# Second MLP in two phases, seven block products in both, hidden outputs in DRAM, low parts of the weights on GpSimd

## The chip, the cores and the metric

One core of a Trainium2 chip. The metric is the device time of one execution in microseconds; three runs of the kernel before gave 2306.87, 2307.96 and 2309.41 us, median 2307.96.

## What is computed

A trunk of two layers on x (1024 tokens by 1024 channels, float32). Only the end of layer 2 concerns this change:

```python
h = rms_norm(x, norm2_gain[i]) * (1 + scale2) + shift2
x = x + gate2 * squared_relu_mlp(h, mlp_w1[i], mlp_w2[i])
# squared_relu_mlp: jnp.square(jax.nn.relu(h @ w1)) @ w2, w1 is 1024x4096, w2 is 4096x1024
```

## The kernel before

All tensors lie with channels on the 128 partitions and tokens along the free dimension: `x` is 8 blocks of 128 channels by 1024 tokens. A float32 product is made of three matmuls on operands rounded to float32r: high part of the weights by high part of the input, high by low, low by high. ACT makes a high part (a copy to float32r), and POOL (GpSimd) or DVE makes the low part as the float32 value less the high one. `T.matmul` always has a 128x128 weight block and 512 tokens (a half).

A "unit" is 128 output channels: 8 blocks of input by 2 halves by 3, so 48 matmuls (`products`, L1564). The hidden layer of 4096 is worked in four groups of 1024 channels, each as two half-groups (`half_group`, L1909). A half-group computes four units of the hidden layer plainly (192 matmuls), squares them (`quad`, L1342), and multiplies these 512 hidden channels by w2 into x: for each of four pairs of output blocks (`DOWN_PAIRS`) seven block products instead of eight (`down_products`, L1874), each 2 weight blocks by 3 matmuls, so 168. The seven products are those of Winograd's form of Strassen's algorithm: quadrants of weights, B11 and so on of the input, and sums of them (S of weights, T of inputs). DVE adds each product as it ends into `x` (`down_evacuate`, L1389). POOL makes the four sums of weight quadrants and all low parts (`down_sums`, L455, `down_low`, L470). Weights come by SP's queue into two slots of `w_raw`.

The second MLP has no other work in it; the last half-group (`end=True`) is written out by hand. Before it `closing` (L1002) normalises the tokens and writes `h_hi` and `h_lo`; the end is SP's store of `out` (L424).

## Time and profile before

| | |
|---|---|
| median of three runs | 2307.96 us |
| profiled execution, its span | 2306.2 us |
| PE busy, matmuls | 98%, 10252 |
| DVE, ACT, POOL busy | 55%, 31%, 35% |
| second MLP, start to last matmul | about 1632 to 2301 us |
| PEclk in it | full speed |

The span runs from the first to the last instruction; the runs are timed around it, so they lie some 2 us above. A DMA row gives the time from issue to landing. PE's matmuls overlap in their pipeline: what one costs is the distance between starts, not its duration. A waiting engine is charged to whoever released it last.

### The profile page before, as it was taken

The numbers are of one execution on the slowest core, as the hardware profiler recorded it, in microseconds if no ns is written. First come the engines' busy times: TensorE is split into PE (matmuls) and PEld (weight loads), VectorE is DVE, ScalarE is ACT, GpSimd is POOL, SyncE is SP. The second block draws the span as 40 slices with busy tenths as digits, with TensorE's granted clock in tenths as the row PEclk, the third lists the DMA queues.
The fourth block names the chain that finished last, engine by engine and source line by source line (L and its number), as shares of the span: only waits on it lengthen the run. The fifth ranks groups of instructions, "written<-read, shape, count | busy, mean of one in ns | idle before, by whom it ended". The sixth has DMA issues, their size and how long they took to land.

```text
span 2306.2 us, 29119 instructions
## 1 busy us (share of the span) xinstructions
PE 2270.8 (98%) x10252; PEld 1812.3 (79%) x10252; DVE 1279.7 (55%) x1641; ACT 711.8 (31%) x978; POOL 803.4 (35%) x622
## 2 busy tenths in 40 slices
PE   7999999999999999999999999999999999999999
PEld 4786787888888888787888888888788888888887
DVE  8689687565565554564334421456554455545455
ACT  4328433223223222233222211224323323322322
POOL 0124403464454452301221112121154455355355
PEclk7999999999999999999999999999999999999999
DMA  6363521212212313223334221222111111111112
GB/s 259 121 185 88 210 92 70 86 55 82 86 51 83 99 55 101 86 87 119 129 118 133 84 72 46 83 73 91 56 49 43 55 55 40 51 55 45 46 64 92
DMA packets 84299, 201.38 MB, mean 87 GB/s; under 512 B 23937, under 2 KB 29953, under 8 KB 83714
## 3 DMA queue, kind: packets, MB, share of 16 engines
q1 hardware_dynamic: 65826, 139.70, 18.9%
q10 hardware_dynamic: 18400, 60.69, 7.5%
q8 instruction: 47, 0.77, 0.1%
q14 instruction: 26, 0.21, 0.0%
HBM read 182.54 MB, written 16.78 MB: 86 GB/s over the span
## 4 chain that ended last, share of the span: by engine, by line
PE 59%; issue 34%; POOL 5%; DVE 0%; POOLq 0%; ACT 0%
PE pp L1570 36%; PE pp L1894 23%; POOL w_lo L432 4%; POOL pr L446 1%; PE pp L1701 0%; POOL w_lo L473 0%; DVE w_lo L1024 0%; PE pp L1680 0%; POOLq L499 0%; DVE x L1398 0%; PE pp L1710 0%; POOLq L431 0%; DVE c_f L1353 0%; ACT w_hi L742 0%; ACT root L533 0%
## 5 line engine op out<-in xcount | busy, mean ns | idle before, releaser
L432 POOL TENSOR_TENSOR w_lo<-w_raw,w_hi 128x1024 fp32r<-128x1024 f32 x136 | 329.9, 2425 | 1186.8 <-ACT w_hi L518 1186.8
L1570 PE MATMUL pp<-h_hi,w_hi 128*128 128x512 f32 x1824 | 602.7, 400 | 15.5 <-DVE h_lo L1166 6.2
L1570 PE MATMUL pp<-h_lo,w_hi 128*128 128x512 f32 x1824 | 594.6, 396 | 0.0
L1570 PE MATMUL pp<-h_hi,w_lo 128*128 128x512 f32 x1824 | 594.5, 396 | 0.0
L1398 DVE SCALAR_TENSOR_TENSOR x<-pp,mod,x 128x512 f32<-128x512 f32 x392 | 294.4, 751 | 278.0 <-PE pp L1894 278.0
L1570 PEld LDWEIGHTS pp<-h_hi,w_hi 128*128 128x128 f32 x1824 | 339.2, 188 | 105.9 <-DVE h_lo L1052 12.9
L1570 PEld LDWEIGHTS pp<-h_hi,w_lo 128*128 128x128 f32 x1824 | 343.2, 188 | 83.2
L1570 PEld LDWEIGHTS pp<-h_lo,w_hi 128*128 128x128 f32 x1824 | 343.3, 188 | 81.2
L518 ACT ACTIVATE w_hi<-w_raw 128x1024 fp32r<-128x1024 f32 x162 | 171.5, 1058 | 615.2 <-PE pp L1570 448.0
L1894 PE MATMUL pp<-c_hi,w_hi 128*128 128x512 f32 x784 | 310.1, 396 | 0.4 <-DVE x L1398 0.4
L1894 PE MATMUL pp<-c_hi,w_lo 128*128 128x512 f32 x784 | 310.1, 396 | 0.0
L1894 PE MATMUL pp<-c_lo,w_hi 128*128 128x512 f32 x784 | 310.1, 395 | 0.0
L473 POOL TENSOR_TENSOR w_lo<-s_w,w_hi 128x768 fp32r<-128x768 f32 x112 | 143.6, 1297 | 135.3 <-ACT w_hi L742 135.2
L1346 DVE SCALAR_TENSOR_TENSOR c_f<-pp,tmp 128x512 f32<-128x512 f32 x84 | 55.5, 688 | 235.9 <-ACT tmp L749 233.5
L1894 PEld LDWEIGHTS pp<-c_hi,w_hi 128*128 128x128 f32 x784 | 147.3, 188 | 36.4 <-issue 0.8
L1894 PEld LDWEIGHTS pp<-c_lo,w_hi 128*128 128x128 f32 x784 | 147.3, 188 | 35.7
L1894 PEld LDWEIGHTS pp<-c_hi,w_lo 128*128 128x128 f32 x784 | 147.3, 188 | 35.6
L473 POOL TENSOR_TENSOR w_lo<-w_raw,w_hi 128x256 fp32r<-128x256 f32 x112 | 114.3, 1020 | 121.2 <-ACT w_hi L742 117.9
L742 ACT ACTIVATE w_hi<-s_w 128x768 fp32r<-128x768 f32 x112 | 70.9, 634 | 238.7 <-PE pp L1894 177.5
L1570 PE MATMUL pp<-hid_hi,w_hi 128*128 128x512 f32 x384 | 142.3, 398 | 1.6 <-POOL w_lo L432 1.6
L1570 PE MATMUL pp<-hid_hi,w_lo 128*128 128x512 f32 x384 | 141.6, 395 | 0.0
L1570 PE MATMUL pp<-hid_lo,w_hi 128*128 128x512 f32 x384 | 141.5, 395 | 0.0
(185 smaller groups left out, 2207.6 us busy)
## 6 DMA issues: line engine op xcount, KB each, us to landing
w_raw<-weights SPq DMA_DIRECT2D x218, 512.0 KB, 3.6
mod_t<-mod_w ACTq DMA_DIRECT2D x64, 512.0 KB, 4.1
mod_first<-mod_w SPq DMA_DIRECT2D x16, 512.0 KB, 15.3
mod_late<-mod_w ACTq DMA_DIRECT2D x2, 4096.0 KB, 23.3
v_dram<-v_out ACTq DMA_DIRECT2D x16, 512.0 KB, 5.5
vf<-v_dram ACTq DMA_DIRECT2D x16, 512.0 KB, 3.3
x<-x_in SPq DMA_DIRECT2D x4, 1024.0 KB, 8.1
qf<-q_dram SPq DMA_DIRECT2D x32, 128.0 KB, 2.5
```

Of the source, the lines that this page charges most:

```text
L432: nc.gpsimd.tensor_tensor(out=w_lo[:, s, :, :], in0=w_raw[:, s, :, :], in1=w_hi[:, s, :, :].bitcast(f32), op=ALU.subtract).then_inc(lo_don ...
L446: nc.gpsimd.tensor_tensor(out=pr[:, b, :, 0:P], in0=pr[:, b, :, 0:P], in1=small[:, b, 3, :].unsqueeze(2).to_broadcast([P, 4, P]), op=ALU.m ...
L473: nc.gpsimd.tensor_tensor(out=down_target(w_lo, part, end), in0=down_source(part, q), in1=down_target(w_hi, part, end).bitcast(f32), op=AL ...
L518: nc.scalar.activation(w_hi[:, s, :, :], w_raw[:, s, :, :], ACT.Copy).then_inc(hi_done, 1)
L742: nc.scalar.activation(down_target(w_hi, part, end), down_source(part, q), ACT.Copy).then_inc(d_hi, 1)
L1346: V.scalar_tensor_tensor(out=out, in0=src[:, columns_of(half)], scalar=0.0, in1=tmp[:, s, columns_of(half)], op0=ALU.max, op1=ALU.mult).th ...
L1398: V.scalar_tensor_tensor(out=xn, in0=banks[BANK[t]], scalar=mod[:, 6 * layer + GATE2, 2 * q + m:2 * q + m + 1], in1=xn, op0=ALU.mult, op1= ...
L1570: last = T.matmul((pp[s] if tile is None else tile)[:, cs], w[:, s, k, :], r[:, k, cs], start=(k == 0 and w is w_hi and r is hi), stop=(k ...
L1894: last = T.matmul(banks[BANK[t]], w[:, slot, k, :], r[:, i, OPERAND[t], :], start=(t in FRESH and i == 0 and w is w_hi and r is c_hi), sto ...
```

## The change

The second MLP is cut in two phases. The first computes the whole hidden layer, all 16 pairs of units (j = 0 to 15), and the second multiplies by w2. Pairs 0 and 1 are computed plainly, as before; pairs 2 to 15 (n = 0 to 13) by seven products, each of 4 weight blocks by 3 matmuls. Then come 16 pairs n = 14 to 29 for w2, four for each group of 1024 hidden channels, again by seven products of 12 matmuls.

The seven input combinations are kept as float32, high and low part. In the first phase they come from h (`combine_inputs`: one DVE instruction on 2048 elements per partition and twelve on 512, all with two inputs in SBUF). A pair's result is squared and combined to the seven inputs of the second phase, each stored to DRAM (`hid_dram`, 256 KB each, `save_pair`) and, at the start of each group, loaded again (`group_operand`): seven loads of 1 MB in pieces of 2 KB, issued by ACT at the seven products of the pair before (n = 13, 17, 21, 25). Each load overwrites the low part that the product has just finished with; ACT then makes the high part and DVE the low part in place (`operand_low`), 2048 elements per partition each.

A pair's weights are 1 MB in four quadrants of 256 KB in `w_raw`. POOL makes four sums and seven low parts, each of 512 elements per partition, in the order: sum S3, low parts 5 and 6 of the pair before, low 0, sums S1, S2, S4, low parts 1 to 4. `w_hi` and `w_lo` hold four products' weights. The quadrant A22 of the next pair is loaded only when low part 6 has been made, and S1 needs it.

In the first phase ACT also copies three partial products out of PSUM and makes three relus for each pair. The loops are written out; the first MLP is unchanged. `scaled` of the last normalisation writes a tile of its own (`g_f`), so it no longer waits for the low part two blocks back.

```diff
+O_B11, O_T1, O_T2, O_B22, O_T3, O_B21, O_T4, O_B12 = range(8)
+OUTPUTS = 7
+QUADS = 4
+UP_PAIRS = MLP_GROUPS * QUADS
+PLAIN_PAIRS = 2
+FAST_UP = UP_PAIRS - PLAIN_PAIRS
+FAST_PAIRS = FAST_UP + MLP_GROUPS * DOWN_PAIRS
+A11, A12, A21, A22 = range(4)
+S_1, S_2, S_4, S_3 = range(4)
+SUM_OF = {S_3: 1, S_1: 2, S_2: 3, S_4: 4}
+PLACED = ((0, 0, 0), (1, 0, 0), (1, 4, 1), (0, 4, 1), (1, 0, 1), (0, 4, 0), (1, 4, 0))
+PREPARED = {1: 1, 2: 2, 4: 3, 6: 4}
...
+        def operand(t, what):
+            turned, row, half = PLACED[t]
+            if what == "f":
+                return wide_f[:, 1 + turned, row:row + QUADS, columns_of(half)]
+            tile = {"hi": (h_hi, hid_lo), "lo": (h_lo, hid_hi)}[what][turned]
+            return tile[:, row:row + QUADS, columns_of(half)]
+        def output(j, o):
+            if j == 0:
+                return wide_f[:, 3, o, columns_of(1 - o // QUADS)]
+            return wide_f[:, o // QUADS, o % QUADS, columns_of(1)]
+        def product_banks(n):
+            return (pp[n % 2][:, 0:HALF], pp[n % 2][:, HALF:], pp[2][:, columns_of(n % 2)])
+        copied = (tmp[:, 1, 0:HALF], tmp[:, 1, HALF:], tmp[:, 0, 0:HALF])
+        rectified = (mod_acc[:, 0:HALF], mod_acc[:, HALF:], tmp[:, 0, HALF:])
...
+        def last_of_group(n):
+            return FAST_UP - 1 <= n < FAST_PAIRS - 1 and (n - FAST_UP) % DOWN_PAIRS == DOWN_PAIRS - 1
...
+            def load_early(n):
+                if n:
+                    sp.wait_ge(w_sum, 4 * (n - 1) + SUM_OF[S_2])
+                    sp.wait_ge(w_low_p, PRODUCTS * (n - 1) + 1)
+                load_quad(n, A11)
+                load_quad(n, A21)
+            def load_late(n):
+                sp.wait_ge(w_sum, 4 * (n - 1) + SUM_OF[S_4])
+                sp.wait_ge(w_low_p, PRODUCTS * (n - 1) + 6)
+                load_quad(n, A12)
+                sp.wait_ge(w_low_p, PRODUCTS * (n - 1) + 7)
+                load_quad(n, A22)
+            def save_pair(j):
+                for counter, count, o in ((u_quad, 2, O_B22), (u_diff, 1, O_T3), (u_quad, 3, O_B11), (u_diff, 2, O_T1),
+                                          (u_diff, 3, O_T2), (u_quad, 4, O_B21), (u_diff, 4, O_T4)):
+                    sp.wait_ge(counter, 4 * j + count)
+                    sp.dma_start(hid_dram[j, o], output(j, o)).then_inc(hid_out, 16)
+            def load_fast():
+                first = U_MLP[1] // 2
+                for pair in range(PLAIN_PAIRS):
+                    for s in range(2):
+                        sp.wait_ge(lo_done, 2 * (first + pair) + s - 1)
+                        sp.dma_start(w_raw[:, s, :, :], weights[up_row(pair, s)]).then_inc(raw_in[s], 16)
+                sp.wait_ge(lo_done, 2 * (first + PLAIN_PAIRS) - 1)
+                load_quad(0, A11)
+                load_quad(0, A12)
+                sp.wait_ge(lo_done, 2 * (first + PLAIN_PAIRS))
+                load_quad(0, A21)
+                load_quad(0, A22)
+                save_pair(0)
+                load_early(1)
+                save_pair(1)
+                for n in range(FAST_PAIRS):
+                    if n + 1 < FAST_PAIRS:
+                        load_late(n + 1)
+                    if n + 2 < FAST_PAIRS:
+                        load_early(n + 2)
+                    if n < FAST_UP:
+                        save_pair(n + PLAIN_PAIRS)
...
+            def weight_low(n, t):
+                pool.wait_ge(w_high, PRODUCTS * n + t + 1)
+                nc.gpsimd.tensor_tensor(out=weight_quad(w_lo, n, t), in0=weight_source(t),
+                                        in1=weight_quad(w_hi, n, t).bitcast(f32), op=ALU.subtract).then_inc(w_low_p, 1)
+            def fast_weights():
+                first = U_MLP[1] // 2
+                for pair in range(1, PLAIN_PAIRS):
+                    for s in range(2):
+                        split_lo(first + pair, s)
+                for n in range(FAST_PAIRS):
+                    sum_of(n, S_3)
+                    if n:
+                        weight_low(n - 1, 5)
+                        weight_low(n - 1, 6)
+                    weight_low(n, 0)
+                    for r in (S_1, S_2, S_4):
+                        sum_of(n, r)
+                    for t in range(1, QUADS + 1):
+                        weight_low(n, t)
+                weight_low(FAST_PAIRS - 1, 5)
+                weight_low(FAST_PAIRS - 1, 6)
...
+            def weight_high(n, t):
+                quad = {0: A11, 5: A12, 6: A22}
+                if t in quad:
+                    act.wait_ge(quad_in[quad[t]], 16 * n + 16)
+                else:
+                    act.wait_ge(w_sum, 4 * n + SUM_OF[(None, S_1, S_2, S_4, S_3)[t]])
+                before = PRODUCTS * n + t - QUADS
+                if before >= 0:
+                    act.wait_ge(f_mm, before + 1)
+                else:
+                    act.wait_ge(gemm, U_MLP[1] + 2 * PLAIN_PAIRS - 1 + t // 2)
+                nc.scalar.activation(weight_quad(w_hi, n, t), weight_source(t), ACT.Copy).then_inc(w_high, 1)
...
+            def fast_mlp():
+                first = U_MLP[1] // 2
+                act.wait_ge(gemm, 2 * first + 1)
+                split_hi(first + 1, 0)
+                rectify(tmp[:, 0, :], pp[3][:, :])
+                act.wait_ge(gemm, 2 * first + 2)
+                split_hi(first + 1, 1)
+                rectify(tmp[:, 1, :], pp[0][:, :])
+                for t, sums in ((1, 1), (2, 9)):
+                    act.wait_ge(t_sum, sums)
+                    operand_high(t)
+                weight_high(0, 0)
+                weight_high(0, 1)
+                act.wait_ge(hid_out, 16 * OUTPUTS)
+                for t, sums in ((4, 5), (6, 13)):
+                    act.wait_ge(t_sum, sums)
+                    operand_high(t)
+                act.wait_ge(u_quad, 4)
+                rectify(tmp[:, 0, :], pp[1][:, :])
+                act.wait_ge(gemm, 2 * first + 4)
+                weight_high(0, 2)
+                rectify(mod_acc[:, :], pp[2][:, :])
+                weight_high(0, 3)
+                for n in range(FAST_PAIRS):
+                    banks = product_banks(n)
+                    up = n < FAST_UP
+                    for t in range(PRODUCTS):
+                        after = PRODUCTS * n + t + QUADS
+                        if up and t < 3:
+                            act.wait_ge(f_mm, PRODUCTS * n + t + 1)
+                            if t == 0 and n:
+                                act.wait_ge(f_sum, 3 * n)
+                            if t == 2 and n == 0:
+                                act.wait_ge(u_quad, 8)
+                            nc.scalar.activation(copied[t], banks[(0, 1, 0)[t]], ACT.Copy).then_inc(f_copy, 1)
+                        if last_of_group(n):
+                            b = group_after(n)
+                            act.wait_ge(f_mm, PRODUCTS * n + t + 1)
+                            if t == 0:
+                                act.wait_ge(hid_out, 16 * OUTPUTS * QUADS * (b + 1))
+                            act.dma_start(operand(t, "f"), hid_dram[QUADS * b:QUADS * b + QUADS, t].rearrange("j p s -> p j s")).then_inc(op_in[t], 16)
+                        if after < PRODUCTS * FAST_PAIRS:
+                            weight_high(after // PRODUCTS, after % PRODUCTS)
+                        if up and t == 3:
+                            act.wait_ge(f_sum, 3 * n + 1)
+                            rectify(rectified[0], banks[1])
+                        if up and t == 5:
+                            act.wait_ge(f_sum, 3 * n + 3)
+                            rectify(rectified[1], banks[2])
+                        if up and t == 6:
+                            act.wait_ge(f_mm, PRODUCTS * n + t + 1)
+                            rectify(rectified[2], banks[0])
+                        if last_of_group(n) and t >= 3:
+                            group_operand(group_after(n), t - 3)
+                        if n and last_of_group(n - 1) and t < 3:
+                            group_operand(group_after(n - 1), t + 4)
+            fast_mlp()
...
+            def up_step(n):
+                j = n + PLAIN_PAIRS
+                banks = product_banks(n)
+                relus = 2 * PLAIN_PAIRS + 3 * n
+                def add(t, out, bank, copy):
+                    dve.wait_ge(f_mm, PRODUCTS * n + t + 1)
+                    V.tensor_tensor(out=out, in0=bank, in1=copied[copy], op=ALU.add).then_inc(f_sum, 1)
+                dve.wait_ge(f_copy, 3 * n + 3)
+                add(3, banks[1], banks[1], 2)
+                dve.wait_ge(hid_out, 16 * OUTPUTS * j)
+                dve.wait_ge(f_relu, relus + 1)
+                squared(j, O_B12, banks[1], rectified[0])
+                add(4, copied[1], banks[0], 1)
+                dve.wait_ge(f_sum, 3 * n + 2)
+                squared(j, O_B22, copied[1], copied[1])
+                dve.wait_ge(u_quad, 4 * j + 2)
+                output_diff(j, O_T3, O_B22, O_B12)
+                add(5, banks[2], banks[2], 0)
+                dve.wait_ge(f_relu, relus + 2)
+                squared(j, O_B11, banks[2], rectified[1])
+                late_diffs(j)
+                dve.wait_ge(f_relu, relus + 3)
+                squared(j, O_B21, banks[0], rectified[2])
+                last_diff(j)
+            def down_step(n):
+                d = n - FAST_UP
+                q = d % DOWN_PAIRS
+                banks = product_banks(n)
+                for t in range(PRODUCTS):
+                    m, half = WRITES[t]
+                    xn = x[:, 2 * q + m, columns_of(half)]
+                    if t in AFTER:
+                        dve.wait_ge(x_ev, PRODUCTS * d + AFTER[t])
+                    dve.wait_ge(f_mm, PRODUCTS * n + t + 1)
+                    V.scalar_tensor_tensor(out=xn, in0=banks[BANK[t]], scalar=mod[:, 6 + GATE2, 2 * q + m:2 * q + m + 1],
+                                           in1=xn, op0=ALU.mult, op1=ALU.add).then_inc(x_ev, 1)
+                    if last_of_group(n) and t >= 4:
+                        operand_low(t - 4)
+                    if last_of_group(n - 1) and t < 4:
+                        operand_low(t + 3)
...
+            def fast_products(n, t):
+                up = n < FAST_UP
+                pe.wait_ge(w_low_p, PRODUCTS * n + t + 1)
+                if n == 0 and t in PREPARED:
+                    pe.wait_ge(op_low, PREPARED[t])
+                if n and last_of_group(n - 1):
+                    pe.wait_ge(op_low, len(PREPARED) + PRODUCTS * group_after(n - 1) + t + 1)
+                if t == 0 and n < FAST_UP + 2:
+                    pe.wait_ge(u_quad, 4 * n + 4)
+                elif t == 0:
+                    pe.wait_ge(x_ev, PRODUCTS * (n - 2 - FAST_UP) + PRODUCTS)
+                elif t == 5 and n == 0:
+                    pe.wait_ge(u_quad, 8)
+                elif t in (2, 3, 4) and up:
+                    pe.wait_ge(f_copy, 3 * n + t - 1)
+                elif t == 6 and up:
+                    pe.wait_ge(f_sum, 3 * n + 2)
+                elif t in (2, 3, 4, 6):
+                    pe.wait_ge(x_ev, PRODUCTS * (n - FAST_UP) + {2: 1, 3: 2, 4: 3, 6: 5}[t])
+                bank = product_banks(n)[BANK[t]]
+                hi, lo = operand(t, "hi"), operand(t, "lo")
+                high, low = weight_quad(w_hi, n, t), weight_quad(w_lo, n, t)
+                for i in range(QUADS):
+                    for w, r in ((high, hi), (high, lo), (low, hi)):
+                        last = T.matmul(bank, w[:, i, :], r[:, i, :], start=(t in FRESH and i == 0 and w is high and r is hi),
+                                        stop=(i == QUADS - 1 and w is low), skip_group_check=t not in FRESH)
+                last.then_inc(f_mm, 1)
+            first = U_MLP[1] // 2
+            opening_pair(first, 3, (pp[3], pp[0]))
+            pe.wait_ge(evac[1], first)
+            plain_unit(first + 1, 0, pp[1])
+            plain_unit(first + 1, 1, pp[2])
+            for n in range(FAST_PAIRS):
+                for t in range(PRODUCTS):
+                    fast_products(n, t)
 # ---- launch: one core
```

## Rows read from the trace of the kernel before

**Rows 1.** The page: span, and busy time, share and instructions of each engine.
```profile
span 2306.2 us, 29119 instructions
...
PE 2270.8 (98%) x10252; PEld 1812.3 (79%) x10252; DVE 1279.7 (55%) x1641; ACT 711.8 (31%) x978; POOL 803.4 (35%) x622
```

**Rows 2.** Stretch 1650 to 2250, in the second MLP: busy us (instructions), PEclk, DMA share.
```profile
1650.00:2250.00 600.00, 599.47 (x2569) 482.66 (x2570) 303.58 (x375) 176.75 (x230) 287.31 (x258) 1.00 0.16 51
```

**Rows 3.** PE's waits, 1630 to 2301: total us, times, longest.
```profile
PE pp L1570 <- DVE h_lo L1052: 1.7, 3, 0.7
PE pp L1570 <- POOL w_lo L432: 1.0, 1, 1.0
```

**Rows 4.** PE in order of time: start, duration, line.
```profile
1699.40 0.40 PE L1894 MATMUL pp<-c_hi,w_lo 128*128 128x512 f32 x1
...
1700.80 0.40 PE L1894 MATMUL pp<-c_hi,w_lo 128*128 128x512 f32 x1
```

**Rows 5.** POOL by shape, 1650 to 2250: busy us, mean ns | idle before.
```profile
L432 POOL TENSOR_TENSOR w_lo<-w_raw,w_hi 128x1024 fp32r<-128x1024 f32 x30 | 72.4, 2415 | 239.9 <-ACT w_hi L518 239.9
...
L473 POOL TENSOR_TENSOR w_lo<-w_raw,w_hi 128x512 fp32r<-128x512 f32 x28 | 36.1, 1288 | 30.2 <-ACT w_hi L742 30.2
...
L473 POOL TENSOR_TENSOR w_lo<-s_w,w_hi 128x256 fp32r<-128x256 f32 x28 | 20.7, 738 | 53.8 <-ACT w_hi L742 53.8
```

**Rows 6.** ACT by shape, the same stretch.
```profile
L518 ACT ACTIVATE w_hi<-w_raw 128x1024 fp32r<-128x1024 f32 x29 | 30.7, 1060 | 145.7 <-PE pp L1570 87.7 <-PE pp L1894 58.0
...
L742 ACT ACTIVATE w_hi<-w_raw 128x512 fp32r<-128x512 f32 x28 | 17.6, 628 | 50.0 <-PE pp L1894 50.0
```

**Rows 7.** DVE by shape, whole span.
```profile
L1398 DVE SCALAR_TENSOR_TENSOR x<-pp,mod,x 128x512 f32<-128x512 f32 x392 | 294.4, 751 | 278.0 <-PE pp L1894 278.0
...
L1346 DVE SCALAR_TENSOR_TENSOR c_f<-pp,tmp 128x512 f32<-128x512 f32 x84 | 55.5, 688 | 235.9 <-ACT tmp L749 233.5 <-ACT tmp L754 2.5
...
L1353 DVE TENSOR_TENSOR c_f<-c_f 128x512 f32<-128x512 f32 x55 | 37.7, 686 | 1.1
...
L1024 DVE TENSOR_TENSOR w_lo<-w_raw,w_hi 128x1024 fp32r<-128x1024 f32 x24 | 29.4, 1224 | 12.8 <-ACT w_hi L518 12.8
...
L965 DVE SCALAR_TENSOR_TENSOR mod_acc<-mod_late,cond,mod_acc 128x1024 f32<-128x1024 f32 x16 | 20.5, 1279 | 0.4 <-DMA mod_late<-mod_w 0.2
```

**Rows 8.** DVE in order of time, at 92.
```profile
92.37 3.41 DVE L965 SCALAR_TENSOR_TENSOR mod_acc<-mod_t,cond,mod_acc 128x1024 f32<-128x1024 f32 x1
```

**Rows 9.** POOL in order of time, at 92.
```profile
92.08 2.62 POOL L432 TENSOR_TENSOR w_lo<-w_raw,w_hi 128x1024 fp32r<-128x1024 f32 x1 [14.49 <-ACT w_hi L518]
```

**Rows 10.** DVE in order of time, 550 to 553.
```profile
550.14 3.44 DVE L965 SCALAR_TENSOR_TENSOR mod_acc<-mod_t,cond,mod_acc 128x1024 f32<-128x1024 f32 x2
```

**Rows 11.** POOL in order of time, 550 to 554.
```profile
550.77 1.72 POOL L465 TENSOR_TENSOR s_w<-s_w,w_raw 128x256 f32<-128x256 f32 x1
552.57 1.60 POOL L467 TENSOR_TENSOR s_w<-w_raw,s_w 128x256 f32<-128x256 f32 x1
```

**Rows 12.** Stretches: one 2 KB-piece load (1781 to 1784); a queue of large loads (255 to 275).
```profile
1781.00:1784.00 3.00, 3.00 (x14) 2.41 (x14) 1.67 (x3) 0.17 (x1) 2.79 (x4) 1.00 0.56 180
255.00:275.00 20.00, 19.90 (x85) 15.74 (x86) 12.45 (x11) 5.88 (x8) 7.96 (x4) 1.00 1.02 410
```

**Rows 13.** DMA issues: KB each, median us to landing.
```profile
w_raw<-weights SPq DMA_DIRECT2D x218, 512.0 KB, 3.6
...
out<-x SPq DMA_DIRECT2D x16, 256.0 KB, 3.1
```

**Rows 14.** Loads of w_raw issued from 250 to 285.
```profile
DMA to landing us min/median/max: 3.5/6.9/8.5
```

**Rows 15.** ACT's queue at 250: two DMA issues.
```profile
250.00 1.02 ACTq L728 DMA_DIRECT2D mod_late<-mod_w  x2
```

**Rows 16.** DVE at the end of the opening.
```profile
1644.64 0.75 DVE L1052 SCALAR_TENSOR_TENSOR h_lo<-tmp,mod,h_hi 128x512 fp32r<-128x512 f32 x1 [0.32 <-ACT h_hi L557]
```

More of the change, by code:

```diff
@@ L346, in load_mlp, with part @@
                 sp.wait_ge(lo_done, U_MLP[layer] + 1)
-                def part(g, h, end=False):
-                    for r in (2, 3) if end else (2, 3, 4):
+                def part(g, h):
+                    for r in (2, 3, 4):
                         load_up(layer, g, h, r)
                     for q in range(DOWN_PAIRS):
-                        load_down(layer, g, h, q, end)
-                    if not end:
-                        load_up(layer, g, h, 5)
+                        load_down(layer, g, h, q)
+                    load_up(layer, g, h, 5)
                 with sp.Fori(0, FAST) as g:
@@ L480, in half_group @@
                     split_lo(pair + 1, 1)
-                    if not end:
-                        split_lo(pair + 2, 0)
+                    split_lo(pair + 2, 0)
                     for q in range(DOWN_PAIRS):
@@ L485, in half_group @@
                         for part in range(4):
-                            down_low(layer, g, h, q, part, end)
-                    if not end:
-                        split_lo(pair + 2, 1)
+                            down_low(layer, g, h, q, part)
+                    split_lo(pair + 2, 1)
                 with pool.Fori(0, FAST) as g:
@@ L730, in _, with down_high @@
             closing(U_WO // 2, 1)
-            def down_high(layer, g, h, q, part, end=False):
+            def down_high(layer, g, h, q, part):
                 if part in (0, 3):
@@ L740, in down_high @@
                 else:
-                    act.wait_ge(gemm, mlp_pair(layer, g, h) * 2 + ((3, 5) if end else (4, 5))[part // 2])
-                nc.scalar.activation(down_target(w_hi, part, end), down_source(part, q), ACT.Copy).then_inc(d_hi, 1)
+                    act.wait_ge(gemm, mlp_pair(layer, g, h) * 2 + (4, 5)[part // 2])
+                nc.scalar.activation(down_target(w_hi, part), down_source(part, q), ACT.Copy).then_inc(d_hi, 1)
             def up_relu(layer, g, h, r):
@@ L795, in half_group @@
                     act.wait_ge(gemm, pair * 2 + 3)
-                    if not end:
-                        split_hi(pair + 2, 0)
+                    split_hi(pair + 2, 0)
                     up_relu(layer, g, h, 2)
@@ L1340, in _, with quad @@
             closing(U_WO // 2, 1, GATE1, late=True)
-            def quad(layer, g, h, r, half, out, counter, end=False):
+            def quad(layer, g, h, r, half, out, counter):
                 s = r % 2
-                src = pp[3] if r == 0 or end else pp[1 - s]
+                src = pp[3] if r == 0 else pp[1 - s]
                 V.scalar_tensor_tensor(out=out, in0=src[:, columns_of(half)], scalar=0.0, in1=tmp[:, s, columns_of(half)],
@@ L1440, in half_group @@
                     step(g, h, 3)
[L1441 to L1444 removed]
+                    odd_unit(layer, g, h, 1)
                     if h and layer == 0:
                         mod_part(g + 6, pp[2])
[L1447 removed]
+                    for q in range(DOWN_PAIRS):
                         down_evacuate(layer, g, h, q)
@@ new lines, in _ @@
+            combine_inputs()
+            plain_outputs(0, (pp[3], pp[0]), (tmp[:, 0, :], tmp[:, 1, :]))
+            operand_low(1)
+            dve.wait_ge(t_sum, 13)
+            for t in (2, 4, 6):
+                operand_low(t)
+            plain_outputs(1, (pp[1], pp[2]), (tmp[:, 0, :], mod_acc[:, :]))
+            for n in range(FAST_UP):
+                up_step(n)
+                if last_of_group(n):
+                    for t in range(3):
+                        operand_low(t)
+            for n in range(FAST_UP, FAST_PAIRS):
+                down_step(n)
@@ L1990, in _, with plain_unit @@
                           hooks={2: lambda: blend(kb * KC + 7, 1, kb, 3)})
-            mlp(1)
+            def plain_unit(pair, s, tile):
+                pe.wait_ge(lo_done, 2 * pair + s + 1)
+                for k in range(KC):
+                    last = products(s, k, h_hi, h_lo, tile=tile)
+                last.then_inc(gemm, 1)
+            def fast_products(n, t):
[33 more added lines that the diff above has]
+                    fast_products(n, t)
 def kernel(x, c, positions, norm1_gain, norm2_gain, mod_w, mod_b, swa_w_qkv, swa_q_gain, swa_k_gain,
```

285 lines of the change are left out of this document (163 added, 122 removed).

## Prediction

> **What bounds the kernel now.** I read the page's busy shares first: PE 98%, the others 31 to 55% [rows 1]. Then the second MLP alone, since nothing else changes: in 600 us of it PE is busy 599.5, at full granted clock, with POOL at 48%, DVE at 51% and the DMA engines at 16% [rows 2]. PE's waits between 1630 and 2301 come to some 3 us, 1.7 for the normalised input and 1.0 for one POOL low part [rows 3]. So the stage is a chain of matmuls, and its time is their number by their distance: six starts take 1.40 us, 0.2333 us each [rows 4]. A change pays if it removes matmuls and adds no wait.
>
> **What it removes.** Before: 32 units of 48 and 8 half-groups of 168, 2880 matmuls. After: 4 x 48 + 14 x 84 + 16 x 84 = 2712. 168 fewer at 0.2333 are 39.2 us. The few small PE stalls after 1660 (0.6 us) go too, and the opening loop of DVE loses a drain of some 0.15 us for each of seven blocks, 1.0 us. Clock: 1.00 before [rows 2], and PE stays as busy, so nothing there.
>
> **One pair in the new stage.** A product is 12 x 0.2333 = 2.8 us, a pair 19.6. POOL: 11 instructions of 512 elements at 1.29 [rows 5], 14.2 us. ACT in the first phase: seven high parts, three copies and three relus at 0.63 [rows 6], 8.2 us. DVE there: 11 instructions at 0.69, 7.6 us; down: seven at 0.75, 5.3 us [rows 7]. DMA: 1.05 MB of weights and 1.84 MB of stores in 19.6 us are 147 GB/s, where the trace moved 410 [rows 12]. No engine is over its time; what counts is the order.
>
> **POOL's chain.** Count from the first matmul of a pair. Product 2 ends at 8.4; copy 0.63, high part 6 0.63, low part 6 1.29: 11.0. Only now is A22 of the next pair loaded. 256 KB took 3.1 us, 512 KB 3.6 [rows 13]; with 3.1, it lands at 14.1. Three sums and low part 1 are 5.2: 19.3, needed at 22.4. Spare: 3.1 us.
>
> **POOL and DVE together.** A DVE instruction with two SBUF inputs that takes 1.28 us (the `mod_late` row) [rows 7] took 3.41 when a POOL instruction had begun 0.3 us earlier, and ended 1.1 us after it [rows 8, 9]; two of them took 3.44 together while POOL's 0.74 us instructions [rows 5] took 1.72 and 1.60 [rows 10, 11]. So the two alternate, and a round costs about 1.68 instead of 1.28 + 0.74 = 2.02: full exclusion, less 0.34. The adds from PSUM stay at 0.75 in the midst of POOL's work [rows 7]. The Trainium skill, "SBUF — State Buffer", section Who interferes with whom, says the same: the pair of ports is an exclusive lock for a DVE instruction with two SBUF inputs against a GpSimd one that reads SBUF, and whoever comes second fully blocks; by that rule the second phase's boundaries below pay, and without it they would cost about 2 us each. The trace agrees with it.
> First phase: five such DVE instructions in a pair (one square, four differences). POOL 14.2 + 5 x 0.69 = 17.6 of 19.6 us. Two of them fall between A22's landing and low part 1, so the spare shrinks from 3.1 to some 2 us. No stall, with a margin that one slower load would take.
> Second phase away from a boundary: no such DVE instruction, no ACT copy. No stall.
>
> **The group boundaries, four.** Here the seven operands (7 x 1.05 MB) are replaced while PE goes on.
> DMA: the nearest row is one 512 KB load in 2 KB pieces: 3 us at share 0.56 and 180 GB/s, so 0.54 MB in 1.68 us, 322 GB/s at full share [rows 12]. 1 MB takes 3.26 us. Seven and the weights' 1 MB are 26.1 us from 4.4 (issue at 2.9 and 1.5 to the first data): the last lands at about 31, is a high part (2048 elements, from 0.628 and 1.060 for 512 and 1024 [rows 6]: 1.92) at 33, a low part (from 0.686 and 1.224 [rows 7]: 2.30) at 35.3, for product 6 of the next pair at 36.4, and before that product an add of 0.75 that stands behind it on DVE. So transfers just fit: 0.3 us to spare.
> Lock: from 14.9 (DVE's first low part, behind the fifth add) to 35.6 it must hold seven DVE low parts, 16.1 us, and ten POOL instructions (S1, S2, S4, low 1 to 4, S3, low 5, low 6), 12.9, less seven overlaps of 0.34: 26.6 us in 20.7. 5.9 us too much. As in-order waits add to that (an add cannot be done before its product, and product 1 waits for low part 1, which stands behind three sums with a DVE low part between each), I take 7 us, bounds 2 (no exclusion) and 12 (load of A22 late as in the burst of large loads, median 6.9 us instead of 3.6 [rows 13, 14], and nothing else hidden). Three such boundaries: 21 us.
> The first (n = 13) is worse. ACT has in that pair seven DMA issues of 0.5 [rows 15], seven high parts, six copies and relus at 0.63 and four operand high parts at 1.92: 19.4 of 19.6 us in one order, so the last relu comes near 25, the last difference at 26.7, and only then DVE's low part 0, ending at 29.0. Product 0 of pair 14 wanted it at 19.6: 9.4 us, and some 1 us more at the end of the seven. 10.5 us, bounds 6 and 16.
> Together 31.5 us.
>
> **The opening.** DVE's last low part of h ends at 1645.4 [rows 16], then it has the combinations (2.3 + 12 x 0.70, and up to 4.4 of POOL's two 2.4 us low parts), the squares of pair 0 (5.6), four operand low parts (9.2) and the squares of pair 1 (5.6): 36 to 41 us. PE reaches product 0 at about 1673 (two plain units, 22.4 us, and the same 1.0 us wait), and wants the last of them, by a copy on ACT, by 1684. I take 3 us, bounds 0 and 6. The end (last adds, stores) is the same instructions: nothing.
>
> **Sum.** -39.2 - 0.6 - 1.0 + 3.0 + 31.5 = -6.3 us on the span of 2306.2: 2299.9. The median of the runs is 1.8 above the profiled span: 2301.7.
>
> **Rivals.**
> (1) The boundaries are hidden: what POOL has made ahead (up to four products) absorbs the exclusion; four boundaries cost 12 instead of 31.5 us: 2282. For it: POOL's low part 1 is up to 3 us early. Against: 26.6 us of work in 20.7.
> (2) Slower: the boundaries are longer than the saving. Place: DVE low parts, POOL's sums and the late A22 in one chain at n = 13, 17, 21 and 25. Price: 12 us at each of three and 16 at the first, 52 in place of 31.5: 2322. It decides for slower once the four exceed 38 us, 9.5 on average. For it: a 512 KB load took up to 8.5 us behind large ones [rows 14], and transfers have 0.3 us to spare: at 250 instead of 322 GB/s the last operand is 6 us late.
> (3) A22 is late in every pair: its landing over 5 us from issue, with the two DVE instructions before low part 1, costs 1 us in each pair for each us beyond: at 6.4 some 1.4 x 28 = 39 us: 2341. Against: the first phase's stores are issued when A22 has landed, and the DMA engines are a third busy.
> (4) The saving is not real, because PE's distance changes between products of 12 matmuls and waits. Against: distance 0.2333 through waits after every 6 [rows 4]. Small chance, within the others.
>
> **Chances.** Forecast 0.50 (2290 to 2310), (1) 0.20, (2) 0.22, (3) with (4) 0.08. The measurement tells 0.2%, 4.6 us, from no change: below 2303.3 lie 0.30 of the forecast and all of (1), 0.50; between, 0.18 of the forecast and 0.02 of (2), 0.20; above 2312.6 0.30. The range leaves out the fastest end of (1) and most of (3): 2276 to 2326.
>
> **What would show it.** The span of the second MLP holds 2712 matmuls at 0.2333. PE's waits: none over 1 us inside the first phase after the opening; at n = 13, 17, 21 and 25 and the pair behind, waits for DVE's `operand_low` and POOL's `weight_low`, 7 us each and 10 at the first. DVE's low parts of 2048 elements mean over 3 us instead of 2.3, and POOL's 512 mean over 1.29 there. ACT waits little for operand loads. If DVE's low parts take 2.3 us at the boundaries, (1) holds; if POOL's S1 waits for A22 in every pair and PE with it, (3).

## The result, and the profile after

The changed kernel takes 2265.7 us (2264.4 to 2266.8, four runs) and the one before, measured beside it, 2308.0 (2306.9 to 2309.4): a ratio of 0.9815, 95% interval 0.9801 to 0.9829. So 42.4 us less, where 6.3 less were forecast. The sign is right, the size is not, and the time lies outside the range.

The page's busy shares, to be held against [rows 1]: span, then busy time, share and instructions of each engine.

```profile
span 2264.2 us, 28332 instructions
...
PE 2192.5 (97%) x10084; PEld 1786.1 (79%) x10084; DVE 1274.9 (56%) x1551; ACT 756.1 (33%) x1054; POOL 991.4 (44%) x668
```

There are 168 matmuls fewer, as counted (10252 to 10084). But PE's busy time fell by 78.3 us, and 168 x 0.2333 is 39.2. Something else made PE's work shorter.

The landmark that is the same work in both kernels is the first `scaled` of half 1 in the last normalisation; ahead of it nothing but the tile that `scaled` writes differs in the code. DVE in order of time (start, duration), first of the kernel before:

```profile
1631.52 1.41 DVE L1044 SCALAR_TENSOR_TENSOR tmp<-x,amp,pp 128x512 f32<-128x512 f32 x2 [2.90 <-PE pp L1710]
```

and of the changed one:

```profile
1595.72 1.41 DVE L1283 SCALAR_TENSOR_TENSOR wide_f<-x,amp,pp 128x512 f32<-128x512 f32 x2 [2.87 <-PE pp L2043]
```

35.8 of the 42.0 us between the two profiled spans were won before the changed part begins. From the landmark to the start of the last matmul it is 669.15 us before (to 2300.67) and 664.85 after (to 2260.57): the second MLP itself gave 4.3 us. That is near the forecast of 6.3, and by luck, as the terms below show. The last 1.9 us lie behind the last matmul: 5.5 us to the end of the span before, 3.6 after. In the kernel before SP had a queue of 16 stores of `out` to issue there, one each 0.69 us, and the last went out 0.9 us after the last add and landed 3.05 us later; in the changed one the last goes out at once and lands after 2.04.

Where the 35.8 us come from is to be seen in two stretches of unchanged and of changed code, 700 to 750 and 1800 to 1850: busy us (instructions) of PE, PEld, DVE, ACT and POOL, then PEclk, DMA share, GB/s. The kernel before:

```profile
700.00:750.00 50.00, 50.00 (x216) 40.26 (x215) 29.59 (x32) 16.59 (x21) 24.45 (x21) 1.00 0.17 55
1800.00:1850.00 50.00, 50.00 (x216) 40.26 (x215) 24.80 (x30) 16.58 (x18) 15.91 (x10) 1.00 0.17 53
```

The changed one:

```profile
700.00:750.00 50.00, 50.00 (x222) 41.40 (x221) 29.75 (x34) 15.12 (x22) 33.42 (x32) 1.00 0.17 52
1800.00:1850.00 50.00, 50.00 (x223) 41.39 (x222) 25.74 (x28) 19.68 (x35) 40.47 (x29) 1.00 0.38 128
```

PE is busy all the time and its granted clock is 1.00 in all four, yet it does 222 or 223 matmuls where it did 216. The distance between two starts fell from 0.2333 us [rows 4] to 0.2267 (26 distances from 2254.67 to 2260.57 in the changed kernel), with the same instruction, the same shape and the same clock, from early in the program on.

The waits of PE in the changed stretch, 1590 to 2264 (total us, times, longest), to be held against [rows 3]:

```profile
PE pp L2343 <- POOL w_lo L651: 22.3, 13, 3.6
PE pp L2343 <- issue: 9.5, 1, 9.5
PE pp L2343 <- ACT tmp L1159: 3.5, 1, 3.5
PE pp L1903 <- POOL w_lo L560: 1.4, 1, 1.4
PE pp L1903 <- DVE h_lo L1291: 0.8, 2, 0.4
```

L2343 is the line of `fast_products`. The 9.5 under "issue" is the first boundary: DVE's first low part (L1788, 1915.50 for 2.28 us) ends at 1917.78 and PE starts at 1917.88. The waits for L651, POOL's `weight_low`, are the boundaries too, since between 1660 and 1905 PE waits for nothing. The distances between starts of L2343, each less 0.2267, summed over a stretch, give what each costs: opening 6.6 us; first phase after it 0.0; boundaries at n = 13, 17, 21 and 25 and the pair behind 16.7, 9.8, 9.9 and 11.6, together 48.0. Only 3.7 of the 6.6 and 31.4 of the 48.0 are waits of over 0.5 us. Of the rest, 19.5 us in all, 14.4 are matmuls that start some 0.43 us apart, and 5.1 are waits of about 0.4 us and the first matmuls behind a wait. PE in order of time at the first boundary:

```profile
1917.88 0.77 PE L2343 MATMUL pp<-h_hi,w_hi 128*128 128x512 f32 x1 [9.54 <-issue]
...
1919.30 0.63 PE L2343 MATMUL pp<-h_hi,w_hi 128*128 128x512 f32 x1
1919.73 0.63 PE L2343 MATMUL pp<-h_lo,w_hi 128*128 128x512 f32 x1
...
1921.65 0.40 PE L2343 MATMUL pp<-h_hi,w_hi 128*128 128x512 f32 x1
1921.88 0.40 PE L2343 MATMUL pp<-h_lo,w_hi 128*128 128x512 f32 x1
```

The granted clock says why, in the same columns as the stretches above: behind the 9.7 us wait, behind the last waits (3.7 us each) of the second and the third boundary, and behind the first wait (3.1 us) of the fourth, where the clock did not fall.

```profile
1917.00:1922.00 5.00, 4.12 (x11) 3.30 (x12) 5.00 (x3) 0.00 (x0) 0.00 (x0) 0.56 1.05 406
...
2022.00:2027.00 5.00, 4.37 (x13) 3.45 (x14) 0.11 (x1) 0.00 (x0) 3.06 (x4) 0.68 0.35 105
...
2108.00:2113.00 5.00, 4.48 (x13) 3.54 (x14) 0.00 (x1) 0.00 (x0) 2.94 (x3) 0.66 0.37 105
...
2178.90:2183.90 5.00, 4.71 (x19) 3.58 (x20) 5.00 (x3) 5.00 (x5) 5.00 (x2) 1.00 0.54 207
```

### The profile page after: what moved, and what is told of

It reads as the page before. It is cut to its first block and busy times, and to the rows that moved or that the text cites. A ratio compares the mean times of both kernels' runs of the same rounds, so it can differ in the third digit from the quotient of the medians.

```text
span 2264.2 us, 28332 instructions
## 1 busy us (share of the span) xinstructions
PE 2192.5 (97%) x10084; PEld 1786.1 (79%) x10084; DVE 1274.9 (56%) x1551; ACT 756.1 (33%) x1054; POOL 991.4 (44%) x668
## 5 line engine op out<-in xcount | busy, mean ns | idle before, releaser
L1903 PEld LDWEIGHTS pp<-h_hi,w_hi 128*128 128x128 f32 x1376 | 254.9, 188 | 77.1 <-DVE h_lo L1291 10.9
L1903 PEld LDWEIGHTS pp<-h_hi,w_lo 128*128 128x128 f32 x1376 | 258.8, 188 | 55.0
L1903 PEld LDWEIGHTS pp<-h_lo,w_hi 128*128 128x128 f32 x1376 | 258.9, 188 | 53.5
L651 POOL TENSOR_TENSOR w_lo<-mod_t,w_hi 128x512 fp32r<-128x512 f32 x120 | 200.9, 1697 | 22.7 <-ACT w_hi L1111 22.5
L2343 PE MATMUL pp<-hid_lo,w_hi 128*128 128x512 f32 x480 | 191.1, 398 | 14.6 <-POOL w_lo L651 11.1
L2343 PE MATMUL pp<-hid_hi,w_hi 128*128 128x512 f32 x480 | 189.5, 395 | 0.0
L2343 PE MATMUL pp<-hid_lo,w_lo 128*128 128x512 f32 x480 | 189.3, 394 | 0.0
L1637 DVE SCALAR_TENSOR_TENSOR x<-pp,mod,x 128x512 f32<-128x512 f32 x168 | 126.1, 751 | 109.7 <-PE pp L2226 109.7
L1865 DVE SCALAR_TENSOR_TENSOR x<-pp,mod,x 128x512 f32<-128x512 f32 x112 | 83.8, 748 | 184.2 <-PE pp L2343 184.2
L2343 PE MATMUL pp<-h_hi,w_hi 128*128 128x512 f32 x360 | 143.8, 399 | 20.7 <-POOL w_lo L651 11.2
L651 POOL TENSOR_TENSOR w_lo<-w_raw,w_hi 128x512 fp32r<-128x512 f32 x90 | 127.4, 1419 | 67.3 <-ACT w_hi L1111 67.3
L1111 ACT ACTIVATE w_hi<-mod_t 128x512 fp32r<-128x512 f32 x120 | 75.5, 630 | 210.2 <-POOL mod_t L646 143.6
L2343 PE MATMUL pp<-h_hi,w_lo 128*128 128x512 f32 x360 | 142.9, 397 | 0.0
L2343 PE MATMUL pp<-h_lo,w_hi 128*128 128x512 f32 x360 | 142.9, 397 | 0.0
L1903 PE MATMUL pp<-hid_hi,w_hi 128*128 128x512 f32 x384 | 140.0, 392 | 1.8 <-POOL w_lo L560 1.8
L1903 PE MATMUL pp<-hid_lo,w_hi 128*128 128x512 f32 x384 | 139.1, 389 | 0.0
```

The lines of the kernel that those rows point to most:

```text
L651: nc.gpsimd.tensor_tensor(out=weight_quad(w_lo, n, t), in0=weight_source(t), in1=weight_quad(w_hi, n, t).bitcast(f32), op=ALU.subtract).th ...
L1111: nc.scalar.activation(weight_quad(w_hi, n, t), weight_source(t), ACT.Copy).then_inc(w_high, 1)
L1637: V.scalar_tensor_tensor(out=xn, in0=banks[BANK[t]], scalar=mod[:, 6 * layer + GATE2, 2 * q + m:2 * q + m + 1], in1=xn, op0=ALU.mult, op1= ...
L1865: V.scalar_tensor_tensor(out=xn, in0=banks[BANK[t]], scalar=mod[:, 6 + GATE2, 2 * q + m:2 * q + m + 1], in1=xn, op0=ALU.mult, op1=ALU.add) ...
L1903: last = T.matmul((pp[s] if tile is None else tile)[:, cs], w[:, s, k, :], r[:, k, cs], start=(k == 0 and w is w_hi and r is hi), stop=(k ...
L2343: last = T.matmul(bank, w[:, i, :], r[:, i, :], start=(t in FRESH and i == 0 and w is high and r is hi), stop=(i == QUADS - 1 and w is low ...
```

## The experiments

Two questions: what shortened every matmul, and whether the boundaries cost what they do for the reason given. For the first, the theory was the place of the operands in SBUF, which is the address at which a tile begins in each partition. The change adds `shift_d`, a tile of 16 bytes per partition, ahead of `mod_first`, `h_hi`, `h_lo` and the other operands of the matmuls. It takes 32 bytes in the program's allocation, so `h_hi` begins at byte 76672 of each partition (a multiple of 128) instead of 76640 (96 beyond one), and all later tiles move with it. The weights (`w_hi` at 57472, `w_lo` at 65664, both multiples of 128) lie ahead of it and stay. Within the weights, and within the moving operands (`h_*`, `c_*`, `hid_*`), tiles and blocks lie multiples of 128 bytes apart, so one number places each group. These addresses are the program's; no trace shows them. The distance from `w_hi` to `h_hi` is the sum of the tiles' sizes, each rounded up to a multiple of 32 bytes. The rival: the changed code has some other effect on the whole program.

**One tile of 32 bytes in the kernel before.** Nothing reads or writes it.

```diff
         shift_b = sb("shift_b", [P, KC])
+        pad = sb("pad", [P, 8])
```

> The kernel before with one unused tile of 32 bytes per partition ahead of mod_first, so that h_hi, h_lo, c_hi, c_lo, hid_hi, hid_lo and all later tiles start at a multiple of 64 bytes, as they do in the changed kernel; nothing else differs. Theory A (the matmul distance of 233.3 ns before and 226.7 ns after is set by where the tiles lie): distance 226.7 ns everywhere, 35.8 us less up to the second MLP as in the changed kernel, and 2880 x 6.67 ns = 19 us less in it: 2253 us. Rival B (the distance belongs to the other instructions of the changed kernel, or to the chip or the day): it stays 233.3 ns and 2308 us.

2254.8 us (2254.0 to 2256.1), ratio 0.9770 (0.9754 to 0.9786). The same stretches of it:

```profile
700.00:750.00 50.00, 50.00 (x223) 41.40 (x222) 29.77 (x34) 15.13 (x22) 33.46 (x32) 1.00 0.15 52
1800.00:1850.00 50.00, 50.00 (x222) 41.41 (x221) 29.30 (x36) 15.01 (x23) 29.15 (x29) 1.00 0.15 44
```

222 to 223 matmuls in 50 us, as in the changed kernel, and 53.4 us from a tile that does nothing. It is also 10.9 us faster than the changed kernel. No instruction of the changed code is in this kernel, so the place is the cause and the rival is out.

**The same tile in the changed kernel**, which takes its operands to 32 beyond a multiple of 128.

```diff
         shift_d = sb("shift_d", [P, QUADS])
+        pad = sb("pad", [P, 8])
```

> The changed kernel with a further unused tile of 32 bytes, so that the same tiles start 32 bytes off a multiple of 64 again. Theory A: distance 233.3 ns, 35.8 us more ahead of the second MLP and up to 2712 x 6.67 ns = 18 us more in it, of which the stalls give a few back: 2311 to 2320 us, the cost or gain of the change without its side effect. Rival B: 2266 us.

2315.8 us (2313.4 to 2318.5), ratio 1.0033 (1.0021 to 1.0044), with 216 matmuls in 50 us again. This is the change alone, measured at the same distance as the kernel before: 7.6 us slower. With both at the short distance (the changed kernel against the first experiment) it is 10.9 slower. At 0.2333 its opening costs 5.5 and its boundaries 14.4, 9.0, 9.0 and 10.2 us. The sum of the prediction with these sizes is -39.2 - 1.6 + 5.5 + 42.6 = +7.3. In the two profiled executions the stage from the landmark to the last matmul is 6.7 us longer, the end 1.9 shorter and all ahead of the landmark 1.3 longer.

**96 bytes instead of 32 in the kernel before**: the moving operands at 64 beyond a multiple of 128.

```diff
+        pad = sb("pad", [P, 24])
```

> As the first, with 96 bytes: the tiles start at a multiple of 64 but 64 bytes off the place, modulo 128, that they have with 32 bytes. If 64 bytes are what counts: 226.7 ns and 2253 us. If it is 128: 233.3 ns and 2308 us.

2273.1 us in one run: between the two cases that had been thought of. Its stretch 1800 to 1850:

```profile
1800.00:1850.00 50.00, 50.00 (x220) 41.01 (x220) 26.04 (x31) 13.85 (x20) 28.56 (x30) 1.00 0.13 42
```

220 matmuls, a distance of 0.2289. So there are three levels, not two.

**The 32 bytes ahead of all tiles** (before `x`): moving operands at a multiple of 128, as in the first experiment, but the weights now 32 beyond one.

```diff
+        pad = sb("pad", [P, 8])
         x = sb("x", [P, KC, S])
```

> The 32 bytes ahead of x, the very first tile: h_hi and later tiles lie as in the first run, but x, w_raw, w_hi and w_lo are now 32 bytes off a multiple of 64. If only the moving operand counts: 226.7 ns and 2253 us. If the weights' place counts as well: over 226.7 ns, about 2308 us.

2307.7 us in one run, distance 0.2333. So it is not the moving operand alone that decides: the weights' place counts as much.

**Both placed apart**: 64 beyond for the weights, a multiple of 256 for the moving operands.

```diff
+        pad0 = sb("pad0", [P, 16])
         x = sb("x", [P, KC, S])
...
         shift_b = sb("shift_b", [P, KC])
+        pad1 = sb("pad1", [P, 24])
```

> 64 unused bytes ahead of x and 96 ahead of mod_first: the moving operands start at a multiple of 128 (and 256), the weights at 64 modulo 128. If weights count as the moving operands do: 228.9 ns and about 2273 us. If for weights 64 is enough: 226.7 ns and 2255 us.

2271.7 us in one run, distance 0.2289: the weights at 64 beyond cost what the moving operands did there.

**Both at multiples of 256.**

```diff
+        pad0 = sb("pad0", [P, 32])
         x = sb("x", [P, KC, S])
...
         shift_b = sb("shift_b", [P, KC])
+        pad1 = sb("pad1", [P, 8])
```

> The kernel before with 128 unused bytes ahead of x and 32 ahead of mod_first: w_hi, h_hi, h_lo, c_hi start at a multiple of 256 (in the first run at 128 modulo 256). So far the distance was 226.7 ns with all operands at multiples of 128, 228.9 with the moving ones at 64 modulo 128, 233.3 with either kind at an odd multiple of 32. If the step of interest ends at 128: 226.7 ns and 2255 us. If 256 gives more: below 226.7 ns, each ns some 9 us.

2253.3 us (2253.2 to 2253.7), ratio 0.9760 (0.9743 to 0.9776), distance 0.2267. The 1.5 us to the first experiment are no gain that the distance shows: a multiple of 128 is enough.

| weights, beyond a multiple of 128 | moving operands | distance |
|---|---|---|
| 0 | 96 (kernel before) | 0.2333 |
| 0 | 32 (changed, padded) | 0.2333 |
| 32 | 0 | 0.2333 |
| 0 | 64 | 0.2289 |
| 64 | 0 | 0.2289 |
| 0 | 0 (changed; before, padded) | 0.2267 |

**The boundaries without the lock.** DVE's low parts of the loaded operands become zeros written by DVE, at the same places and with the same waits. This leaves out the low parts of the seven combinations in the four groups of the second phase. Zeros have no SBUF input, so DVE and POOL need not exclude each other. A write of zeros is also 0.5 us shorter than a low part, 3.6 us over the seven of a boundary; the run does not separate this from the lock.

```diff
+                if op_lows[0] > len(PREPARED):
+                    V.memset(operand(t, "lo").bitcast(f32), 0.0).then_inc(op_low, 1)
+                    return
                 V.tensor_tensor(out=operand(t, "lo"), in0=operand(t, "f"), in1=operand(t, "hi").bitcast(f32),
```

> The changed kernel, but at the four group boundaries DVE fills the low parts of the operands with zeros (no SBUF input) instead of computing them from two SBUF inputs; it leaves out the low parts of the loaded operands. DVE is still occupied for about 1.8 us each instead of 2.3, with the same waits. In the changed kernel the boundaries cost PE 48.0 us over 226.7 ns per matmul (16.7, 9.8, 9.9, 11.6). Theory L (mutual exclusion of DVE and POOL): POOL's low parts at the boundaries fall from 3.3 to 1.3 us, the three later boundaries to 0 to 3 us each, the first keeps most of its 9.7 us wait, as ACT's order sets it: some 20 us left, 2238 us. Rival O (DVE's occupancy and its order of work): the boundaries keep 40 us or more, 2258 us or more.

2235.1 us (2233.1 to 2235.8), 30.6 less than the changed kernel; the boundaries cost 11.7, 1.2, 0.1 and 0.8 us instead of 16.7, 9.8, 9.9 and 11.6. The pair behind the first boundary in the changed kernel, DVE and then POOL:

```profile
1926.07 2.73 DVE L1788 TENSOR_TENSOR hid_hi<-wide_f,hid_lo 128x2048 fp32r<-128x2048 f32 x1
1928.72 0.74 DVE L1865 SCALAR_TENSOR_TENSOR x<-pp,mod,x 128x512 f32<-128x512 f32 x1
1929.38 2.73 DVE L1788 TENSOR_TENSOR h_lo<-wide_f,h_hi 128x2048 fp32r<-128x2048 f32 x1
```

```profile
1923.31 3.34 POOL L651 TENSOR_TENSOR w_lo<-mod_t,w_hi 128x512 fp32r<-128x512 f32 x1 [8.28 <-ACT w_hi L1111]
1926.82 3.14 POOL L646 TENSOR_TENSOR mod_t<-w_raw 128x512 f32<-128x512 f32 x1 [0.17 <-POOL w_lo L651]
1929.92 3.34 POOL L651 TENSOR_TENSOR w_lo<-w_raw,w_hi 128x512 fp32r<-128x512 f32 x1
```

and the same without the lock:

```profile
1925.22 1.76 DVE L1789 MEMSET h_lo<- 128x2048 f32 x1 [0.38 <-issue]
```

```profile
1924.87 1.31 POOL L651 TENSOR_TENSOR w_lo<-mod_t,w_hi 128x512 fp32r<-128x512 f32 x1 [7.97 <-ACT w_hi L1111]
1926.34 1.30 POOL L646 TENSOR_TENSOR mod_t<-w_raw 128x512 f32<-128x512 f32 x1 [0.17 <-POOL w_lo L651]
1927.60 1.31 POOL L651 TENSOR_TENSOR w_lo<-w_raw,w_hi 128x512 fp32r<-128x512 f32 x1
```

POOL's instruction of 512 elements takes 3.34 us beside a low part of DVE and 1.31 beside a write of zeros. One DVE low part and one POOL instruction make a round of 3.3 us (DVE starts 1926.07 and 1929.38). The prediction's terms give 2.30 + 1.29 - 0.34 = 3.25. The Trainium skill, "SBUF — State Buffer", section Who interferes with whom, has this lock for a DVE instruction with two SBUF inputs and not for one without; the trace agrees, 3.34 against 1.31 us.

The loads are late at the boundaries in both kernels. In the changed one the quadrant A22 takes 6.0, 5.7, 4.7 and 6.5 us to land, where loads of this size took 2.9 in the median, and POOL stands idle for it before its sum S1. The load at the first boundary (KB, us to landing), then POOL in order of time at the first and the second:

```profile
w_raw<-weights SPq DMA_DIRECT2D x1, 256.0 KB, 6.0
...
1906.11 1.29 POOL L646 TENSOR_TENSOR mod_t<-w_raw 128x512 f32<-128x512 f32 x1 [3.40 <-issue]
...
1998.70 1.30 POOL L646 TENSOR_TENSOR mod_t<-w_raw 128x512 f32<-128x512 f32 x1 [3.17 <-issue]
```

Without the lock A22 takes 5.2, 4.0 and 4.7 us at the last three, and they cost 1.2 us or less. So late loads alone do not make these boundaries dear. Whether the lock alone would, with A22 in time, was not tried.

Of the first boundary 11.7 us remain, a wait of 10.2 and slow matmuls: it waits for something else. The next run asks whether that is the order of DVE's work.

**Low parts 0 and 1 earlier in pair 13.** DVE makes the first ahead of the square of B11 and the second ahead of the last square, instead of both behind the last difference.

```diff
                 dve.wait_ge(f_relu, relus + 2)
+                if last_of_group(n):
+                    operand_low(0)
                 squared(j, O_B11, banks[2], rectified[1])
                 late_diffs(j)
+                if last_of_group(n):
+                    operand_low(1)
                 dve.wait_ge(f_relu, relus + 3)
...
-                    for t in range(3):
-                        operand_low(t)
+                    operand_low(2)
```

> The changed kernel with DVE's first two operand low parts of the first boundary taken ahead of the last squares and differences of pair 13, in the 6 us in which DVE waited for a PSUM result or a relu, instead of behind them. Theory: the wait of 9.7 us at product 0 of pair 14 goes down by 5 to 8 us (DVE's low part 0 is ready before product 0 wants it, the next wait is POOL's or low part 2), so 2258 to 2261 us. Rival: what is won there comes back as waits for POOL, since its low parts are behind too: 2264 to 2266 us.

2263.5 us (2262.9 to 2265.9), 2.2 less, hardly more than the runs of either vary. PE's waits in it, from 1590:

```profile
PE pp L2346 <- POOL w_lo L651: 19.4, 14, 3.6
PE pp L2346 <- issue: 5.6, 1, 5.6
PE pp L2346 <- ACT tmp L1159: 3.5, 1, 3.5
PE pp L2346 <- DVE x L1869: 3.0, 1, 3.0
```

The wait for the first operand is 5.6 instead of 9.5 us, but one of 3.0 for DVE appears, ending some 12 us after the first. The boundary went from 16.7 to 14.9 only, short of what was expected. One reason is the edit itself: it puts low part 0 behind the wait for the second relu, not into it. Its high part was there at 1904.34, but DVE stood idle from 1907.08 to 1911.95:

```profile
1911.95 2.64 DVE L1788 TENSOR_TENSOR h_lo<-wide_f,h_hi 128x2048 fp32r<-128x2048 f32 x1 [4.87 <-ACT mod_acc L1114]
```

So this run does not show that DVE's order sets the first wait. In the changed kernel the trace shows the chain ahead of it: POOL's sum S1, held up for A22 (above), then S1's high part on ACT, the second relu behind it, and the square on DVE.

```profile
1907.42 0.63 ACT L1111 ACTIVATE w_hi<-mod_t 128x512 fp32r<-128x512 f32 x1 [3.81 <-POOL mod_t L646]
...
1910.28 0.57 ACT L1114 ACTIVATE mod_acc<-pp 128x512 f32<-128x512 f32 x1
```

```profile
1910.89 0.69 DVE L1793 SCALAR_TENSOR_TENSOR wide_f<-pp,mod_acc 128x512 f32<-128x512 f32 x1 [4.53 <-ACT mod_acc L1114]
```

What this relu reads was ready at 1906.36, and POOL had stood idle 3.4 us for A22, so with A22 in time the relu and all behind it could have come up to 3.4 us earlier: an estimate that no run tested.

**Low parts in four instructions of 512 elements**, to let POOL in between.

```diff
-                V.tensor_tensor(out=operand(t, "lo"), in0=operand(t, "f"), in1=operand(t, "hi").bitcast(f32),
-                                op=ALU.subtract).then_inc(op_low, 1)
+                for i in range(QUADS):
+                    last = V.tensor_tensor(out=operand(t, "lo")[:, i, :], in0=operand(t, "f")[:, i, :],
+                                           in1=operand(t, "hi")[:, i, :].bitcast(f32), op=ALU.subtract)
+                last.then_inc(op_low, 1)
```

> The changed kernel with each operand low part on DVE made by four instructions of 512 elements instead of one of 2048. PE waits at the boundaries for POOL, which waits up to 2.1 us for each DVE instruction. Theory L: POOL gets between the pieces, its instructions fall from 3.3 to about 1.9 us, DVE's low parts take longer in sum (4 x 1.9 us while POOL has work). The sum of work under the lock grows by the three fixed costs. I expect PE's waits to move from POOL to DVE, and the time within 6 us of 2266. Rival O: POOL's durations don't change, 2266 us plus some 3 us.

2290.0 us (2286.5 to 2292.0), 24.3 more: much worse than expected. The boundaries cost 66.0 us instead of 48.0. The low parts of the opening are split too, and it costs 9.7 instead of 6.6. DVE and POOL from 1900 on (count | busy, mean ns | idle before), and PE's waits:

```profile
L1789 DVE TENSOR_TENSOR hid_hi<-wide_f,hid_lo 128x512 fp32r<-128x512 f32 x64 | 66.4, 1096 | 6.3 <-ACT hid_lo L1117 6.3
...
L651 POOL TENSOR_TENSOR w_lo<-mod_t,w_hi 128x512 fp32r<-128x512 f32 x64 | 89.5, 1413 | 46.1 <-ACT w_hi L1111 45.9
```

```profile
PE pp L2345 <- DVE x L1867: 15.2, 8, 4.4
PE pp L2345 <- DVE hid_hi L1789: 13.7, 3, 5.1
```

POOL is near its own 1.29 us again, but DVE pays: a low part is now 4 x 1.06 in the mean, some 4.2 us, instead of 2.6. The wait went over to DVE, as expected, and the queue behind it (the add that frees a bank) with it.

## Why the prediction was right or wrong

**The step that failed: the distance of the matmuls.** The sum took 0.2333 us [rows 4] as a constant of the instruction, and rival (4), the only one that asked whether the distance changes, was put down to "small chance" from a row that only showed that it doesn't change with waits. It was a property of where the tiles began. The sum had no term for it: every matmul, those ahead of the stage too, started 6.7 ns earlier behind the one before, 35.8 us ahead of the stage and 19.2 in it; the 168 saved are then worth 38.1 and not 39.2. The diff showed a new tile ahead of the operands; the prediction does not mention it. Worked out from the runs, the second MLP is -38.1 (fewer matmuls) - 19.2 (2880 x 0.0067) + 48.0 (boundaries) + 6.6 (opening) - 1.6 (stalls of before that went, as forecast; it closes the sum) = -4.3. 35.8 us came ahead of it and 1.9 behind it. That the time fell at all is luck too: with the operands placed as badly as before, the change is 7.6 us slower.

**The boundaries: lock and places right, size wrong.** Forecast 31.5, measured 48.0 at the short distance (42.6 at the old one). The waits alone are 31.4: 12.4 at the first against 10.5, 6.1, 6.1 and 6.8 against 7. They wait for `weight_low` and at the first for `operand_low`, at the four places named. The lock is needed for them at the last three: with zeros in place of the low parts 1.2, 0.1 and 0.8 us are left. What was missing is the term for the clock, next.

At the first boundary the times came as forecast (last relu at 24.5 of the pair against 25, last difference at 26.4 against 26.7, low part 0 at 28.6 against 29.0), but in part by luck. The forecast had ACT full for 19.4 of 19.6 us. ACT stood idle 3.8 us for POOL's sum, as A22 landed 6.0 us after its issue and not 3.1. Rival (2) had a late A22; the forecast had not.

**"PE stays as busy, so nothing there" was wrong.** Behind seven of the eight waits at the boundaries, of 2.4 to 9.7 us each, and behind that of the opening, the granted clock is 0.50 to 0.68 over 5 us, and some ten matmuls start 0.43 us apart, the distance of the lower level, 1.2 GHz. Behind the eighth, 3.1 us, it stayed at 1.00. Over boundaries and opening 48.0 - 31.4 + 6.6 - 3.7 = 19.5 us lie outside the waits, 14.4 of them in matmuls at the lower level. At the boundaries a wait cost about 1.5 times its length, all in all. With that term the sum of the prediction would have been +13; at the old distance boundaries and opening came to 48.1 instead of 54.6, and the second experiment measured +7.6: slower, the side of rival (2) (+14). Its condition, four boundaries over 38 us, was met.

**The opening:** 3 forecast, 3.7 of wait for the copy on ACT (L1159) that stands behind DVE's squares, as said, 1.6 for the clock and 1.3 for two short waits for POOL and the matmuls behind the waits. The wait's nearness is luck. The forecast's terms for DVE add up to 31 to 35.5 us and not to the 36 to 41 it gives; by them DVE is done before PE wants the result. DVE took 43 (1607.6 to 1650.7): its four low parts stood beside POOL's and took 13.3 us, not 9.2.

**The end:** put at nothing, measured 1.9 us less. The adds are the same, but the stores no longer queue on SP.

**First phase: right.** 0.0 us beyond the distance from the opening to n = 13. In the pairs n = 0 to 12 no load of weights took over 4.3 us and behind 1656 POOL stood idle for 0.8 us at most before a sum, so rival (3) is out. At the four boundaries A22 was late.

**Signs.** DVE's low parts of 2048 elements were to mean over 3 us; at the boundaries they take 2.28 us alone and up to 2.73 beside POOL, 2.6 in the mean (3.4 in the opening), while POOL's 512 elements go from 1.29 to 3.34, as said. As the starts read, DVE waits only for what is left of POOL's instruction, and POOL for the whole of DVE's. The length of the round was right, which of the two shows it was not.

## What to carry to other kernels

Before costing an edit, look at what it does to the addresses of the operands of the bounding engine, and compare a stretch of code that the edit doesn't touch: its matmul count per 50 us tells at once whether a gain is the edit's. Here the edit alone costs 7.6 us, and 32 bytes of padding in the old kernel, 53.4 us, beat it. And where PE is the bound, price a wait of some us with what follows it (here half its length again, most of it matmuls at the lower clock), not by its length alone. When an experiment moves work into a gap, look in its trace whether the work stands in the gap or behind it.

## What the runs showed of the hardware

The start-to-start distance of a float32r matmul of 128x128 by 512 was 0.2267 us when weights and moving operand both begin at a multiple of 128 bytes in the partition, 0.2289 when one kind is 64 bytes off, 0.2333 when the moving operand is 32 or 96 off or the weights 32. At 2.4 GHz these are 544, 549 and 560 cycles. At the lower clock the place made no difference: 0.427 us, 512 cycles at 1.2 GHz, in the changed kernel and in the second experiment, with its moving operands 32 off. 256 gives nothing beyond 128. The 8976 float32r matmuls of this kind in the kernel before, times 6.7 ns, are 59.8 us; 53.4 were gained, and in which stretches the rest is lost was not followed up. What in the chip makes the difference is not shown; both kinds off at once, and single tiles off, were not tried.

The lock between DVE and POOL holds for the length of one instruction of either. A DVE instruction of 512 elements takes 0.68 us alone and up to 1.78 beside POOL (1.02 to 1.10 in the mean); one of 2048 elements stretches POOL's from 1.29 to 3.34. A write of zeros by DVE takes 1.76 us for 2048 elements, and POOL's instructions beside it stayed at 1.30 to 1.31.
